# Routed experts computed two at a time, 64 tokens each, with rows fetched and scattered by index

## The reference

```python
def hierarchical_moe(h, w_rg, b_rg, w_re, b_re, w_gate, w_up, w_down):
    ...
    g_idx = jnp.argmax(g_logits, axis=-1)                  # one of 4 groups
    top_val, top_idx = lax.top_k(e_in_group, TOP_K_INNER)  # 2 of its 8 experts
    ...
    for e in range(N_EXPERTS):                             # 32
        hid = jax.nn.silu(tok @ w_gate[e]) * (tok @ w_up[e])
        out = out + combine[:, e:e + 1] * (hid @ w_down[e])
```

## Time and profile before

| what | us |
|---|---|
| median of three runs | 3181.31 |
| the profiled execution | 3184.2 |
| its span, first to last instruction | 3182.1 |
| `stage_route`, dispatch and set-up of the experts (2637 to 2697) | 60 |
| `stage_experts`, PE's first to last work (2697 to 3120) | 423 |
| from there to the first weighing of answers (3132.5) | 12 |

### The profile page before, as it was taken

One profiled execution on the slowest core, in us unless ns is written; L12 is line 12 of the kernel. 1 busy time (PEld: TensorE's weight loads), 2 busy tenths in 40 slices (PEclk: granted clock), 3 DMA queues, 4 the chain that ended last, 5 costly groups with the idle time before them and its releaser, 6 DMA issues. The chain is left out here.

```text
span 3182.1 us, 46953 instructions
## 1 busy us (share of the span) xinstructions
PE 2522.2 (79%) x17448; PEld 1584.8 (50%) x17448; DVE 1910.4 (60%) x3916; ACT 1216.2 (38%) x2728; POOL 1026.9 (32%) x741
## 2 busy tenths in 40 slices
PE   6998799977867777777777777776986973999994
PEld 3444599855722223222222223223875853777772
DVE  6574456443376667666766676654328333787774
ACT  2113533233333333333333333323334332888781
POOL 0000100031054555555555555552005211323371
PEclk9998899988999999999999999998996685999997
DMA  9842000031199999999999999993651004999992
GB/s 371 319 146 102 24 4 5 4 109 54 66 417 421 422 420 413 417 414 417 415 416 413 415 415 413 417 418 133 228 185 37 2 1 178 360 397 402 386 381 93
DMA packets 178115, 847.15 MB, mean 266 GB/s; under 512 B 23760, under 2 KB 37600, under 8 KB 96352
## 3 DMA queue, kind: packets, MB, share of 16 engines
q0 software_dynamic: 84208, 587.76, 45.0%
q1 hardware_dynamic: 75568, 220.55, 18.4%
q10 hardware_dynamic: 18112, 35.85, 3.1%
HBM read 794.82 MB, written 47.19 MB: 265 GB/s over the span
## 5 line engine op out<-in xcount | busy, mean ns | idle before, releaser
L1867 PE MATMUL bank<-expert_rows,mixed 128*128 128x512 f32 x1024 | 483.9, 617 | 181.2 <-ACT mixed L1825 179.3
L1867 PE MATMUL bank<-peer_q,mixed 128*128 128x512 f32 x1024 | 479.2, 612 | 162.6 <-ACT mixed L1825 162.6
L1753 POOL DMA_INDIRECT expert_rows<-in_uv,expert_idx x256 | 343.3, 1341 | 406.5 <-PE bank L1867 211.2
L1753 POOL DMA_INDIRECT peer_q<-in_uv,expert_idx x256 | 340.6, 1330 | 299.3 <-PE bank L1867 243.8
L1783 DVE SCALAR_TENSOR_TENSOR expert_rows<-expert_rows,h_rows 128x1024 f32<-128x1024 f32 x256 | 313.7, 1225 | 203.9 <-DMA expert_rows<-in_uv,expert_idx 203.7
L1783 DVE SCALAR_TENSOR_TENSOR peer_q<-peer_q,h_rows 128x1024 f32<-128x1024 f32 x256 | 313.8, 1226 | 202.3 <-DMA peer_q<-in_uv,expert_idx 202.3
L1867 PEld LDWEIGHTS bank<-expert_rows,mixed 128*128 128x128 f32 x1024 | 188.6, 194 | 475.4 <-ACT mixed L1825 257.1
L1867 PEld LDWEIGHTS bank<-peer_q,mixed 128*128 128x128 f32 x1024 | 186.8, 192 | 452.8 <-ACT mixed L1825 263.9
L1814 ACT ACTIVATE expert_act<-expert_dot 128x2 f32<-128x2 f32 x256 | 52.1, 203 | 866.4 <-DVE peer_q L1783 394.7
L2886 DVE TENSOR_TENSOR expert_lo<-expert_w,expert_hi 128x1024 fp32r<-128x1024 f32 x195 | 250.7, 1334 | 58.3 <-ACT expert_hi L2847 58.3
L518 DVE TENSOR_TENSOR w_lo<-weight_slots,w_hi 128x384 fp32r<-128x384 f32 (+3 forms) x152 | 106.5, 707 | 212.9 <-ACT w_hi L510 212.9
(11 more groups left out here) (457 smaller groups left out, 4420.3 us busy)
## 6 DMA issues: line engine op xcount, KB each, us to landing
expert_w<-in_experts SPq DMA_DIRECT2D x96, 1024.0 KB, 9.7
mod_w<-in_ada_w ACTq DMA_DIRECT2D x17, 2048.0 KB, 11.1
tile_tokens<-dispatched SPq DMA_DIRECT2D x39, 512.0 KB
answered<-tile_y SPq DMA_DIRECT2D x39, 512.0 KB, 5.4
dispatched<-x POOLq DMA_DIRECT2D x9, 2048.0 KB, 7.5
mod_w<-in_ada_w SPq DMA_DIRECT2D x7, 2048.0 KB, 16.7
weight_slots<-in_w_in SPq DMA_DIRECT2D x6, 2048.0 KB, 18.1
weight_slots<-in_w_in SPq DMA_DIRECT2D x8, 1536.0 KB, 6.7
```

The lines of the kernel that those rows point to most:

```text
L1753: pool.indirect_dma_start(rows[n % SLOTS], None, core.dram["uv"], bass.IndirectOffsetOnAxis(idx[:, t, column:column + 1], 0)).then_inc(arr ...
L1867: mm = pe.matmul(bank[2 * (t % 2) + half][:, :], diag[:, j, :], rows[j][:, D + half * S:D + half * S + S], start=column == 0, stop=column ...
```

## The change

Experts get 24 pairs of tiles of 64 places in place of 39 tiles of 128. The first expert of a pair uses columns 0 to 63 of PE's array and PSUM partitions 0 to 63, the second the other half. 8 pairs are two experts' own tiles; 16 pairs are one expert's own tile and one extra tile, which belongs to whatever expert has over 64 tokens, or to none. Weights and tokens are no longer split: PE multiplies them as plain fp32, so a pair takes 16 gate and up products and 8 down products, in twos on the column halves. `stage_route` also works out, for each place of each pair, which row of `h_rows_kept` it takes and which row of `answered` it gives, with 8 more small matmuls; it stores `h_rows` to DRAM from ACT's queue. Empty places have indices beyond the bound. The scatter block and the fill of `dispatched` are gone. In `stage_experts` POOL fetches the tokens of each pair, scatters its answers and fetches the extra tiles' weights, all by index with a bound; SP loads the other weights into a ring of 14 slots. `stage_combine` reads `answered` in order, with four plain DMAs on SP.

```diff
-MOE_T = 128
-MOE_EXTRA = (2 * S - 1) // MOE_T
-MOE_TILES = N_EXPERTS + MOE_EXTRA
-MOE_RING = 2
+MOE_T = 64
+MOE_PAIRS = (N_EXPERTS + MOE_EXTRA) // 2
+MOE_PLAIN = N_EXPERTS - MOE_EXTRA
-MOE_SLOTS = 8
+MOE_SLOTS = 14
+MOE_RING = 3
+NO_ROW = 4096
...
-    core.answered = nc.dram_tensor("answered", (MOE_TILES * MOE_T, D), F32, kind="Internal").ap()
+    core.h_rows = nc.dram_tensor("h_rows_kept", (S, D), F32, kind="Internal").ap()
+    core.answered = nc.dram_tensor("answered", (2 * S, D), F32, kind="Internal").ap()
...
-                if fill is not None:
-                        m = min(KD // 2, rows.shape[1] - n)
-                        pool.wait_ge(chunk_used, KD * (j * len(items) // len(fills)) + 1)
-                        pool.dma_start(rows[:, n:n + m, :], core.x[:, 0:2 * m, :].rearrange("p k t -> p (k t)").rearrange("p (n d) -> p n d", d=D)).then_inc(slots_filled, 16)
-                    pool.wait_ge(slots_filled, 16 * len(fills))
...
                 first_weights(sp)
+                sp.wait_ge(rows_stored, 16 * TT)
+
+            @block.gpsimd
+            def _(pool):
+                pool.memset(tokens[:, :, :], 0.0)
...
+                pe.wait_ge(spotted, 4 * TT)
+                for j in range(2):
+                    for i in range(TT):
+                        mm = pe.matmul(bank[1][:, 0:MOE_PAIRS], in_tile[:, j, i, :], of_tile[:, j, i, :],
+                                       start=j == 0 and i == 0, stop=j == 1 and i == TT - 1)
+                mm.then_inc(slots_known, 1)
...
+                    if half == 1:
+                        act.wait_ge(h_copied, u + 1)
+                        act.dma_start(core.h_rows[i * P:i * P + P, :], hN[:, i, :]).then_inc(rows_stored, 16)
...
+                step(dve.tensor_copy(rank_no[:, :, :], bank[1][:, 0:TT * N_EXPERTS].rearrange("p (i e) -> p i e", e=N_EXPERTS)))
+                step(dve.tensor_scalar(rank_no[:, :, :], rank_no[:, :, :], S - MOE_T, None, ALU.bitwise_and))
+                step(dve.tensor_scalar(beyond[:, :, :], rank[:, :, :], float(MOE_T), None, ALU.is_ge))
-                for m in range(2, -(-S // MOE_T)):
+                for m in range(2, S // MOE_T):
...
+                step.then(dve.tensor_reduce(place[:, :, :], chosen[:, :, :, :], AX.X, ALU.add))
+                step.then(dve.tensor_copy(place_no[:, 0, :, :], place[:, :, :]))
+                step(dve.tensor_scalar(place_no[:, 1, :, :], place_no[:, 0, :, :], 7, None, ALU.logical_shift_right))
+                step.then(dve.tensor_scalar(place_no[:, 0, :, :], place_no[:, 0, :, :], P - 1, None, ALU.bitwise_and))
+                step.then(dve.tensor_copy(spot[:, :, :, :], place_no[:, :, :, :]))
+                for j in range(2):
+                    for i in range(TT):
+                        dve.tensor_scalar(in_tile[:, j, i, :], column_no, spot[:, 0, j, i:i + 1], None, ALU.is_equal).then_inc(spotted, 1)
+                        dve.tensor_scalar(of_tile[:, j, i, :], pair_no, spot[:, 1, j, i:i + 1], answer_no[:, 2 * i + j:2 * i + j + 1],
+                                          ALU.is_equal, ALU.mult).then_inc(spotted, 1)
...
+                dve.wait_ge(slots_known, 1)
+                step.then(dve.tensor_scalar(of_tile[:, 0, 0, :], bank[1][:, 0:MOE_PAIRS], float(NO_ROW), None, ALU.add))
+                step.then(dve.tensor_copy(answer_row[:, :], of_tile[:, 0, 0, :]))
+                step.then(dve.tensor_scalar(token_row[:, :], answer_row[:, :], 1, None, ALU.logical_shift_right))
...
-                n, u = divmod(m, MOE_UNITS)
-                sp.dma_start(weights[:, m, :], core.dram[f"experts{u}"][n * P:(n + 1) * P, :]).then_inc(w_arrived[m], 16)
+                _, u, e = unit_of(m)
+                sp.dma_start(weights[:, m, :], core.dram[f"experts{u}"][e * P:(e + 1) * P, :]).then_inc(w_arrived[m], 16)
...
-                    for i in range(TT):
-                        for j in range(2):
-                            pool.indirect_dma_start(core.dispatched, bass.IndirectOffsetOnAxis(spot[:, i, j, :], 0),
-                                                    hN[:, i, :], None).then_inc(dispatched, 16)
-                    pool.wait_ge(dispatched, 2 * TT * 16)
...
+def pair_order():
+
+    plain, mixed = MOE_PLAIN // 2, MOE_EXTRA
+    order = list(range(3))
+    rest = iter(range(3, plain))
+    for x in range(mixed):
+        order.append(plain + x)
+        if x % 3 == 2:
+            order += [p for p in [next(rest, None)] if p is not None]
+    return order
+
+
+def unit_of(m):
+
+    n, part = divmod(m, 2 * MOE_UNITS)
+    u, half = divmod(part, 2)
+    pair, plain = pair_order()[n], MOE_PLAIN // 2
+    if pair < plain:
+        return pair, u, 2 * pair + half
+    return pair, u, (MOE_PLAIN + pair - plain) if half == 0 else None
...
+    def used(m):
+
+        n, part = divmod(m, 2 * MOE_UNITS)
+        return MOE_UNITS * n + part // 2 + 1
...
+        turned_bank, gate_up_bank, hid_bank, y_bank = bank[0:2], bank[2:4], bank[4], bank[5:7]
...
+                def gather_tokens(n):
+                    if n >= MOE_RING:
+                        pool.wait_ge(tile_turned, 2 * (n - MOE_RING) + 2)
+                    pool.sem_inc(pool_gate, 1)
+                    pool.indirect_dma_start(tokens[:, n % MOE_RING, :], None, core.h_rows,
+                                            bass.IndirectOffsetOnAxis(token_row[:, order[n]:order[n] + 1], 0),
+                                            bounds_check=S - 1, oob_is_err=False).then_inc(t_arrived[n % MOE_RING], 16)
+
+                def extra_units(n, u):
+
+                    for half in range(2):
+                        m = (n * MOE_UNITS + u) * 2 + half + MOE_SLOTS
+                        if m < N * MOE_UNITS * 2 and not owns(m):
+                            pair, unit, _ = unit_of(m)
+                            x, slot = pair - MOE_PLAIN // 2, m % MOE_SLOTS
+                            pool.wait_ge(unit_used, used(m - MOE_SLOTS))
+                            pool.sem_inc(pool_gate, 1)
+                            pool.indirect_dma_start(weights[:, slot, :], None, core.dram[f"experts{unit}"],
+                                                    bass.IndirectOffsetOnAxis(expert_row[:, x:x + 1], 0),
+                                                    bounds_check=N_EXPERTS * P - 1, oob_is_err=False).then_inc(extra_arrived[slot], 16)
+
+                def scatter(n):
+                    pool.wait_ge(y_copied, 2 * n + 2)
+                    pool.sem_inc(pool_gate, 1)
+                    pool.indirect_dma_start(core.answered, bass.IndirectOffsetOnAxis(answer_row[:, order[n]:order[n] + 1], 0),
+                                            y[:, n % MOE_RING, :], None,
+                                            bounds_check=2 * S - 1, oob_is_err=False).then_inc(stored[n % MOE_RING], 16)
+
+                for n in range(MOE_RING):
+                    gather_tokens(n)
                 for n in range(N):
-                    c = CHUNKS - 1
...
+                    if n + MOE_RING < N:
+                        gather_tokens(n + MOE_RING)
+                    if n >= 1:
+                        extra_units(n - 1, MOE_UNITS - 1)
+                        scatter(n - 1)
+                    for u in range(MOE_UNITS - 1):
+                        extra_units(n, u)
+                scatter(N - 1)
+                for s in range(MOE_RING):
+                    pool.wait_ge(stored[s], 16 * len(range(s, N, MOE_RING)))
...
+                for m in range(MOE_SLOTS, N * MOE_UNITS * 2):
+                    if owns(m):
+                        _, u, e = unit_of(m)
+                        sp.wait_ge(unit_used, used(m - MOE_SLOTS))
+                        sp.dma_start(weights[:, m % MOE_SLOTS, :], core.dram[f"experts{u}"][e * P:(e + 1) * P, :]).then_inc(w_arrived[m % MOE_SLOTS], 16)
...
+                def unit_ready(n, u):
+
+                    for half in range(2):
+                        m = (n * MOE_UNITS + u) * 2 + half
+                        pe.wait_ge((w_arrived if owns(m) else extra_arrived)[m % MOE_SLOTS], arrivals(m))
+                    return [weights[:, ((n * MOE_UNITS + u) * 2 + half) % MOE_SLOTS, :] for half in range(2)]
+
+                def gate_up(n, k):
+                    if k % HALF == 0:
+                        pe.wait_ge(tok_copied, 2 * n + k // HALF + 1)
+                    both = unit_ready(n, k // HALF)
+                    for half in range(2):
+                        mm = pe.matmul(gate_up_bank[n % 2][mine(half), :], tok[:, n % 2, k, mine(half)],
+                                       both[half][:, k % HALF * S:k % HALF * S + S], start=k == 0, stop=k == KD - 1)
+                    if k % HALF == HALF - 1:
+                        mm.then_inc(unit_used, 1)
+
+                def turn_hidden(n):
+                    pe.wait_ge(hidden_ready, n + 1)
+                    for f in range(NF):
```

(48 more changed lines are left out.)

276 lines of the change are left out of this document (70 added, 206 removed).

## The result

The changed kernel takes 3047.6 us, the median of 4 runs (3047.49 to 3048.42). The kernel before took 3180.57 us beside it (4 runs, 3179.26 to 3185.63). The ratio is 0.958, 95% interval 0.9563 to 0.9596. The prediction was 3045 us, between 3022 and 3115.

A forecast was written before the change was run, and what follows sets the result against it. PE bounds the experts' stage, with DMA traffic close behind. Gains of 4.0 before and 133.9 in it, less 1.4 after, make 136.5 us: 3184.2 to 3047.7, less 2.9 for the median, forecast 3045, range 3022 to 3115.

The forecast's parts named there:

- The projection's fill: Second projection: the 20 MB fill on POOL is hidden behind PE, so removing it is worth 0.
- The price of a pair: Experts' stage: 12 product times with halves fully overlapped 10.3 us, turning 1.1, switching 0.45; 11.85 us a pair.
- the term for switching: Experts' stage, PE changing between whole array and column halves, twice a pair: taken as 0.45 us a pair.
- The rival of the issue order: Experts' stage: PE begins passes strictly in order, one pass more per entry into halves; 20.6 us, 3066; chance 0.10.
- serial halves: Experts' stage: column halves run one after the other; 22.1 us a pair, 531 for the stage, 3292; chance 0.07.
- Loading: Experts' stage: stationary loads not hidden beside running products, 3.4 us a pair, 83 in all, 3128; chance 0.08.
- What lies beside it: Experts' stage: PE covers silu and copies; ACT and DVE cannot bound; POOL's indexed DMAs 9.5 of 11.85 us.
- DMA: Experts' stage: 94 MB in some 289 us, 327 GB/s, 335 in the heaviest stretch, under 401; doesn't bound.
- Empty places: Experts' stage, rival: empty places move all the same; 402 us in place of 289, 3158; chance 0.05.
- Before the stage: Routing to PE's first turning: routing 8 us longer, scatter block gone, start at 2693.0; gain 4.0 us.
- The stage's ends: Experts' stage: start 0.9 copy and 2.1 half clock, end 1.1 silu and 0.7 copy; 289.2 with the pairs.
- After the stage: PE's last product to DVE's first weighing: 13.8 us against 12.36; loss 1.4 us.

The follow-up runs named there:

- one-half-first: Kernel after with PE's products issued six of the first column half, then six of the second, down products likewise; 3138.0 us.
- run with moved empties: Kernel after with indices of empty places pointed at existing rows (spare answer rows, last expert's weights), so everything moves; 3165.3 us.
- no-extra-fetch run: Kernel after, still 14 slots, without the 48 indexed fetches of extra weight units and PE's waits for them; 3044.3 us, ratio 0.9563.
- merged kernel: Kernel after with the answers weighed inside the experts' block, loaded into freed weight slots, no block end between; 3037.3 us, ratio 0.9545.

## Why the prediction was right, and where it wasn't

The forecast was 2.6 us off, but that flatters it: ahead of the stage and in it 6.2 us more were gained than predicted, and behind it 5.6 us more were lost. That the two nearly cancel is luck. The sum of the terms, 3047.7, was made against a profiled execution, and the profiled one after took 3047.5; the 2.6 us come from the 2.9 taken off at the end, the distance of the profiled execution before from its median, which the kernel after doesn't have (3047.49 against 3047.6).

*The bound.* PE now sets the pace as predicted: 100% busy at the full clock from 2700 to 2900.

*The projection's fill* was costed at nothing; the run with the fill put back shows nothing in its stretch.

*The price of a pair.* Predicted 11.85 us, measured 11.69 (2708.52, 2720.22, 2731.91, ... for the copies). The passes start 0.43 apart in twos, so full overlap, read off attention's quadrants, held for halves of 128 rows too. The difference is the term for switching: 11.69 - 10.3 - 1.1 = 0.3 us where I took 0.45. The rival of the issue order and that of the serial halves are out by these rows. The serial case, which I had put at 22.1 us a pair, isn't reached even by an order made for it: with one half issued after the other a pair takes 15.2 us (copies from 2715.76 to 3065.97, 23 intervals), since PE reaches ahead. (That rival's 531 us for the stage also left out the 4.8 us of its start and end.)

*Loading.* Each of the 768 loads of gate and up takes 0.137 us, and none shows between passes 0.43 apart. The Trainium skill's page "TensorE: Matmul & The Clock Gate" (Part 3, The mechanism), which gave that rival, lets a load overlap a running product only where their row groups differ. Both halves use all the rows here, and the loads are hidden all the same: the measurement decides against the rule. Further up, that section names the background weight buffer as a second case in which a load is pulled ahead of running products; the hidden loads here would fit that, though no run shows the buffer. The same section says that products start strictly in the order of issue; the one-half-first rows (L2856 at 2836.16 before L2875 at 2836.59) disagree with that as well.

*What lies beside it.* silu, the copies and POOL stay hidden; PE's waits in the stage are 0.9 + 0.7 + 0.5 us beside the first tokens' 8.0. POOL's indexed DMAs take 1.0 us each, under the 1.6 of the earlier trace rows that I took as a ceiling.

*DMA.* The mean was right: the trace has 329 GB/s over the stage's 286.2 us, at a DMA share of 0.86, and 327 were predicted. The heaviest stretch wasn't. I had 335 GB/s for it, and 356 to 369 are measured over 100 us each, because I counted only its 15 units and left out the rows of its four pairs, those of five experts in and out, about 1.3 MB: (15.7 + 1.3) / 46.8 = 364. "DMA doesn't bound" came out true, but at a DMA share of 0.95, with 5% left and not the 16% of 335 against 401. The runs with plain pairs first (17 us) and with 8 slots (77 us) show how little room there is.

*Empty places* move nothing; the rival's 3158 us was a fair price for the other case (3165 measured).

*Before the stage.* Routing's end was put at 2683, and it is 2682.6. POOL's first fetch was put at 2686.9 (2683 + 0.9 + 3.0), measured 2686.44. What failed is the last term, the landing: I took 1.2 + 4.2 to 5.4 us from the issue on, from the eight scatters of the earlier trace rows, and it is 3.4. The run with moved empties gives 4.5, and kernels with the same fetch as here 3.4 to 3.8, so 0.7 to 1.1 of it is that the empty rows of the tile don't move; the remainder, a single DMA on idle engines against eight in a row, is argued only. The gain is 7.2 us, where 4.0 was predicted.

*The stage's ends.* 289.2 us predicted, 286.2 measured. With 0.16 us less a pair that is 3.8 of difference, and 0.8 the other way at start and end. As foreseen the first pair runs at half the clock (granted 0.50 from 2690 to 2696), and the last one has silu's chain uncovered (0.94 and 0.52).

*After the stage* is the step that failed: 13.8 us predicted, 19.3 measured. Term by term: from the copy to the scatter 1.9 us (predicted 1.1), from its issue to its landing 2.6 (1.2 + 4.2), then 7.9 us of POOL's DRAIN, of which my sum had nothing, 1.7 for the block end and the clearing around it (1.5), and 5.2 from SP's first issue to the first weighing (0.4 + 5.4). The missing 7.9 us show as 5.5 only because the landing came out 2.8 shorter than I took it. The kernel before had such DRAINs of POOL in front of me, none of them as busy time: 0.7 us after 8 in its scatter block, 4.9 after 21 in its experts' block, 12.5 in its combining block and 17.6 after the peer experts. The two in the middle lie beside other engines' work there. The number of indexed DMAs in a block, which the change raises to 96, was the thing to ask about. The no-extra-fetch run halves it, and the merged kernel hides it, so this cause is shown.

## What to carry to other kernels

Small stationary tiles can be paired on the column halves of PE at little loss (0.3 us of 11.69 here), and the order of the products has to alternate between the halves: groups of three products on one half already cost 0.9 us a pair. When work moves from plain to indexed DMAs, count them per block: each adds 0.08 us (between 8 and 96 of them, 128 rows each) to POOL's DRAIN at the block's end, after everything has landed, so whatever follows should stand in the same block, behind a semaphore. And when a kernel leaves one bound, work out how near the next one is with all of its traffic in the heaviest stretch, not the mean: here 5% was left, and the order of the pairs held it.
